# A hybrid decoder layer on one core: weights of the first projection summed on chip, norm totals reordered, and ACT's two roundings of a step exchanged

## What is computed

```
h  = rmsnorm(x) * (1 + scale1) + shift1
u, cq, ckv, kr = split(h @ w_in)             # pooling | latents | rotary key
x  = x + gate1 * (concat(pool(u), attention(cq, ckv, kr)) @ w_out)
h2 = rmsnorm(x) * (1 + scale2) + shift2
x  = x + gate2 * (square(relu(h2 @ w_up)) @ w_down)      # width 4096
y  = rmsnorm(x)
```

## Time and profile before

| | us |
|---|---|
| median of 3 runs | 1430.6 (1430.16 to 1432.28) |
| the profiled execution | 1427.27 |
| its span, first to last instruction | 1425.5 |
| mean granted clock of TensorE | 0.965 of full |
| PE busy | 1335.7 (94%) |
| DVE busy | 1020.3 (72%) |
| ACT busy | 676.0 (47%) |
| POOL busy | 428.3 (30%) |

### The profile page before, as it was taken

One profiled execution on the slowest core, in us unless ns is written; L12 is line 12 of the kernel. 1 busy time (PEld: TensorE's weight loads), 2 busy tenths in 40 slices (PEclk: granted clock), 3 DMA queues, 4 the chain that ended last, 5 costly groups with the idle time before them and its releaser, 6 DMA issues. The chain is left out here.

```text
span 1425.5 us, 29271 instructions
## 1 busy us (share of the span) xinstructions
PE 1335.7 (94%) x11700; PEld 1209.0 (85%) x11700; DVE 1020.3 (72%) x1725; ACT 676.0 (47%) x1371; POOL 428.3 (30%) x349
## 2 busy tenths in 40 slices
PE   6999989999989999698889999999999999999987
PEld 4899876666666766598789999999999999999987
DVE  4855766565657764379777797868979698796985
ACT  5421556565512233234556633665346653467344
POOL 0032043222312221444235161432505234163230
PEclk9999999999969999899889999999999999999999
DMA  9712133424666768954037384563647447485204
GB/s 344 275 52 62 78 118 108 135 79 152 195 242 209 252 209 242 259 132 115 17 70 163 102 157 110 117 150 90 148 119 144 123 92 164 98 181 110 40 1 126
DMA packets 95473, 198.88 MB, mean 140 GB/s; under 512 B 14407, under 2 KB 21523, under 8 KB 91107
## 3 DMA queue, kind: packets, MB, share of 16 engines
q0 software_dynamic: 30576, 87.04, 27.3%
q1 hardware_dynamic: 63537, 109.89, 23.5%
q10 hardware_dynamic: 1226, 0.08, 0.1%
HBM read 180.96 MB, written 13.79 MB: 137 GB/s over the span
## 5 line engine op out<-in xcount | busy, mean ns | idle before, releaser
L1321 PE MATMUL psa<-x_hi,w_hi 128*128 128x272 f32 x2016 | 592.9, 294 | 32.9 <-DVE xT L2417 14.1
L1321 PE MATMUL psa<-x_hi,w_lo 128*128 128x272 f32 x2016 | 588.4, 292 | 0.0
L1321 PE MATMUL psa<-x_lo,w_hi 128*128 128x272 f32 x2016 | 587.0, 291 | 0.0
L1321 PEld LDWEIGHTS psa<-x_hi,w_hi 128*128 128x128 f32 x2016 | 387.8, 192 | 37.5 <-issue 27.1
L1321 PEld LDWEIGHTS psa<-x_hi,w_lo 128*128 128x128 f32 x2016 | 387.3, 192 | 0.0
L1321 PEld LDWEIGHTS psa<-x_lo,w_hi 128*128 128x128 f32 x2016 | 386.9, 192 | 0.2
L758 POOL TENSOR_TENSOR w_lo<-quarter,w_hi 128x512 fp32r<-128x512 f32 x168 | 255.4, 1532 | 245.0 <-ACT w_hi L1750 244.7
L1750 ACT ACTIVATE w_hi<-quarter 128x512 fp32r<-128x512 f32 x252 | 156.3, 620 | 0.0
L2417 DVE SCALAR_TENSOR_TENSOR xT<-psa,modT,xT 128x272 f32<-128x272 f32 (+1 forms) x280 | 116.8, 470 | 0.0
L1773 ACT ACTIVATE x_hi<-t_sum 128x544 fp32r<-128x544 f32 x72 | 47.6, 661 | 120.1 <-PE psa L1321 92.3
L1773 ACT ACTIVATE x_hi<-t_tmp 128x544 fp32r<-128x544 f32 x71 | 47.0, 662 | 88.6 <-PE psa L1321 73.9
(11 more groups left out here) (326 smaller groups left out, 2354.6 us busy)
## 6 DMA issues: line engine op xcount, KB each, us to landing
quarter<-in_w_down POOLq DMA_DIRECT2D x21, 1024.0 KB, 10.2
quarter<-in_w_up SPq DMA_DIRECT2D x20, 1024.0 KB, 5.4
quarter<-in_w_down SPq DMA_DIRECT2D x20, 1024.0 KB, 5.6
quarter<-in_w_up POOLq DMA_DIRECT2D x20, 1024.0 KB, 10.4
wmod<-in_w_mod SPq DMA_DIRECT2D x8, 2048.0 KB, 8.2
wm<-in_w_mod SPq DMA_DIRECT2D x4, 2048.0 KB, 20.5
quarter<-in_w_out POOLq DMA_DIRECT2D x6, 1024.0 KB, 10.0
quarter<-in_w_out SPq DMA_DIRECT2D x5, 1024.0 KB, 9.1
```

Source lines behind the costliest of these rows:

```text
L1321: mm = pe.matmul(tail_bank(p, i)[:, 0:HB], a[:, i * P:i * P + P], x[:, HB * p:HB * p + HB], start=(m in OPENS and k == 0 and q == 0), stop ...
```

## The change

It does these things.

1. M3's weights in stage 0: buffer 5 gets A12+A11 alone (one accumulating load in place of three), and POOL adds buffer 0 (A21+A22) to it in four pieces, `w_sum`, behind w_lo of steps 3, 4 and 5; ACT's w_high of M3 waits for them. A11 is added to buffer 0, for M6, behind the last of them.
2. SP's order of loads: buffers 1 and 3 come later, behind x_back, and buffer 5 ahead of buffer 2.
3. The totals: PE sums into banks 0 and 1, which needs two banks empty in place of eight, and makes the step's other units before the two that take those banks. In the last phase the first step comes ahead of the totals, and the turning of tiles moves back by one.
4. DVE: t_begun for stage 0 too; add_squares(2) at step 31 in place of 28.
5. ACT: `high(j)` calls w_high(j) first and x_high(j) second.

```diff
+PARTS[0][5] = ('A12', 'A11')
...
-    def wait_weights(eng, w, m):
+    def wait_weights(eng, w, m, k):
...
-        if len(ADDED[m]) == 1:
+        if w == 0 and m == 'M3':
+            eng.wait_ge(sem("w_sum"), BEFORE["w_sum"] + k + 1)
+        elif len(ADDED[m]) == 1:
...
         sp.wait_ge(sem("pv5"), 20)
         load_weights(0, 0)
-        sp.wait_ge(sem("pv5"), 24)
-        load_weights(0, 1)
         sp.wait_ge(sem("s5_mm"), HALVES - 2)
         sp.dma_start(wuv_all[:, :, :], w_uv.rearrange("(k p) n -> p k n", p=P)).then_inc(sem("wuv_in"), 16)
-        sp.wait_ge(sem("pv5"), 25)
-        load_weights(0, 2)
         sp.wait_ge(sem("pv5"), 26)
         load_weights(0, 5)
-        sp.wait_ge(sem("pv5"), NPAIR * NB)
-        load_weights(0, 3)
+        load_weights(0, 2)
         sp.wait_ge(sem("oT_mm"), NB)
         x_back(0, 1, 0)
         x_back(1, 0, 0)
         sp.wait_ge(sem("at_mm"), 1)
+        load_weights(0, 1)
         x_back(2, 0, 1)
         x_back(3, 1, 1)
+        sp.wait_ge(sem("pv5"), NPAIR * NB)
+        load_weights(0, 3)
...
+        def w_sum(k):
+
+            g.wait_ge(sem("added_in0"), BEFORE["added_in0"] + 16)
+            g.wait_ge(sem("added_in5"), BEFORE["added_in5"] + 16)
+            g.tensor_tensor(quarters[5][:, k, :], quarters[5][:, k, :], quarters[0][:, k, :], ALU.add).then_inc(sem("w_sum"), 1)
...
         add_weights(0, 0, 1)
         add_weights(0, 5, 1)
-        add_weights(0, 5, 2)
         for j in range(STAGES * STEPS):
             w, pos, k, m = place(j)
             if not LOW_ON_DVE[j]:
                 w_low(j)
-            if j == 1:
-                add_weights(0, 5, 3)
+            if j == 3:
+                w_sum(0)
+                w_sum(1)
+            if j == 4:
+                w_sum(2)
+            if j == 5:
+                w_sum(3)
+                wait_low(g, 3)
+                g.wait_ge(sem("w_sum"), BEFORE["w_sum"] + 4)
+                add_weights(0, 0, 2)
...
-            if ORDERS[w] is LATE and m == 'M5':
+            if w and ORDERS[w] is LATE and m == 'M5':
...
-                if k == 0 and p == 0 and i >= 2 and phase in (6, 8):
-                    pe.wait_ge(sem("n_root"), phase // 2 - 2)
...
-        def total(n):
+        def step_with_total(j, n):
 
+            phase = j // 4
             pe.wait_ge(sem("n_sum"), n + 1)
-            pe.wait_ge(sem("unit_kept"), 8 * (6 + 2 * n))
+            pe.wait_ge(sem("unit_kept"), 8 * (phase - 1) + 2)
             for e in range(2):
                 c0 = HT * n + HB * e
-                mm = pe.matmul(bank(6 + e)[:, 0:HB], ones[:, :], h_all[:, 0, c0:c0 + HB], start=True, stop=True)
+                mm = pe.matmul(bank(e)[:, 0:HB], ones[:, :], h_all[:, 0, c0:c0 + HB], start=True, stop=True)
             mm.then_inc(sem("n_total"), 1)
+            wait_low(pe, j)
+            pe.wait_ge(sem("x_low"), j + 1)
+            for i in (2, 3):
+                pe.wait_ge(sem("unit_kept"), 8 * (phase - 1) + i + 1)
+                unit_part(j, 1, i)
+            for i in range(4):
+                pe.wait_ge(sem("unit_kept"), 8 * (phase - 1) + 4 + i + 1)
+                unit_part(j, 0, i)
+            pe.wait_ge(sem("n_root"), n + 1)
+            unit_part(j, 1, 0)
+            return unit_part(j, 1, 1)
...
         last = STAGES * STEPS - 4
+        step(last, 1)
         pe.wait_ge(sem("unit_kept"), 8 * (last // 4))
         tile_totals(0)
-        for k in range(4):
-            step(last + k, 1)
-            if k == 1:
+        for k in range(1, 6):
+            if k < 4:
+                step(last + k, 1)
+            if k == 2:
                 pe.wait_ge(sem("n_root"), 3)
...
         def high(j):
+            w_high(j)
             x_high(j)
-            w_high(j)
...
-                if w < 2:
+                if w == 1:
                     chain(tt(t2, b12, b22, ALU.subtract))
...
-            if w < 2 or m != 'M1':
+            if w == 1 or m != 'M1':
                 return
-            if w % 2 == 0:
+            if w == 0:
+                v.wait_ge(sem("at_mm"), 1)
+            elif w % 2 == 0:
...
-            if j in (20, 24, 28, 32, 244, 248):
-                add_squares((20, 24, 28, 32, 244, 248).index(j))
+            if j in (20, 24, 31, 32, 244, 248):
+                add_squares((20, 24, 31, 32, 244, 248).index(j))
```

More of the change, by code:

```diff
@@ L114 @@
           "g_row_in": "consts", "y_left": "left", "y_right": "right", "h_scaled": "n_t", "h_done": "h_ready",
-          "t_begun": "n_hi", "samples_kept": "tok_root", "g_done": "turned_hi", "left_mm": "turned", "right_mm": "turned_lo"}
+          "t_begun": "n_hi", "w_sum": "split", "samples_kept": "tok_root", "g_done": "turned_hi", "left_mm": "turned", "right_mm": "turned_lo"}
 BEFORE = {name: 16 for name in SHARED}
 BEFORE.update({"added_in0": 0, "added_in5": 0})
-BEFORE.update({"quarter_in5": 128, "added_in2": 64, "added_in3": 64, "added_in4": 48, "x_back0": 64, "x_back1": 64, "y_left": 9, "y_right": 9, "h_scaled": 25, "h_done": 25, "t_begun": 25, "samples_kept": 9, "g_done": 9, "left_mm": 9, "right_mm": 9})
+BEFORE.update({"quarter_in5": 128, "added_in2": 64, "added_in3": 64, "added_in4": 48, "x_back0": 64, "x_back1": 64, "y_left": 9, "y_right": 9, "h_scaled": 25, "h_done": 25, "t_begun": 25, "w_sum": 10, "samples_kept": 9, "g_done": 9, "left_mm": 9, "right_mm": 9})
 def place(j):
@@ L1378, in _ @@
         for j in range(4, 4 * (7 * STAGES - 1)):
[L1379 to L1384, removed]
+            if j in (24, 32):
+                mm = step_with_total(j, j // 8 - 3)
+            else:
+                step(j, 1)
+                mm = step(j, 0)
             if j % 4 < 3:
@@ L1410, in _ @@
         last = STAGES * STEPS - 4
+        step(last, 1)
         pe.wait_ge(sem("unit_kept"), 8 * (last // 4))
         tile_totals(0)
-        for k in range(4):
-            step(last + k, 1)
-            if k == 1:
+        for k in range(1, 6):
+            if k < 4:
+                step(last + k, 1)
+            if k == 2:
                 pe.wait_ge(sem("n_root"), 3)
[L1417 to L1426, removed]
+            if k > 2:
+                pe.wait_ge(sem("y_right"), BEFORE["y_right"] + k - 2)
+            turn_right(k - 1, *FINAL[0][k - 1])
+            if k > 2:
+                pe.wait_ge(sem("y_left"), BEFORE["y_left"] + k - 2)
+            turn_left(k - 1, *FINAL[0][k - 1])
         pe.wait_ge(sem("y_right"), BEFORE["y_right"] + 5)
@@ L1748, in w_high @@
                 act.wait_ge(sem("pv5"), RING_PAIRS[0][j])
-            wait_weights(act, w, m)
+            wait_weights(act, w, m, k)
             act.activation(w_hi[j % 4][:, :], w_piece(j), ACT.Copy).then_inc(sem("w_high"), 1)
@@ L1813, in root @@
                 act.wait_ge(sem("h_scaled"), BEFORE["h_scaled"] + 8)
-            act.activation(rr[:, 0:HB], bank(6)[:, 0:HB], ACT.Sqrt, bias=eps[:, :], scale=1.0 / D)
-            act.activation(rr[:, HB:HT], bank(7)[:, 0:HB], ACT.Sqrt, bias=eps[:, :], scale=1.0 / D).then_inc(sem("n_root"), 1)
+            act.activation(rr[:, 0:HB], bank(0)[:, 0:HB], ACT.Sqrt, bias=eps[:, :], scale=1.0 / D)
+            act.activation(rr[:, HB:HT], bank(1)[:, 0:HB], ACT.Sqrt, bias=eps[:, :], scale=1.0 / D).then_inc(sem("n_root"), 1)
         def shift(half, c):
@@ L2371, in x_sum @@
             elif m == 'M6':
-                if w < 2:
+                if w == 1:
                     chain(tt(t2, b12, b22, ALU.subtract))
                 else:
-                    v.wait_ge(sem("t_begun"), BEFORE["t_begun"] + 4 * (w - 2) + k + 1)
+                    v.wait_ge(sem("t_begun"), BEFORE["t_begun"] + 4 * (w - (w > 1)) + k + 1)
                 s = tt(t2, t2, b11, ALU.subtract)
```

## The result

The changed kernel takes 1440.6 us (median of 11 runs beside 11 of the kernel before, 1427.6): ratio 1.0088, 95% interval 1.0066 to 1.0111, or 9 to 16 us slower. Forecast: 1431.5, range 1422 to 1438. The sign of the sum held, but by luck: it was the small difference of two terms of 17 and 18 us, and the 13 us measured are outside the range. One of the 11 runs, of 1836 us with a mean granted clock of 0.65, was in a slow state and is left out of the ratio. The profiled execution took 1443.06 us.

The account below looks back on a forecast made before the run. TensorE, busy 94% of the span, was taken as the bound, losing time only when idle or at the lower clock. Gains of 13.9 and 1.9 against a loss of 16.7 gave +0.9 on 1430.6: 1431.5 us, range 1422 to 1438.

Parts of the forecast that it names:

- the start: Start of the tail: POOL's wait for accumulating loads before w_lo goes, PE's 8.94 us stand with it; gain 11.4 us.
- 1.5 back at the first hand-over: First hand-over between products: DVE begins to empty banks 1.5 us later against PE, losing that much.
- M6: Third product: t_begun moves four subtractions out of DVE's crowded stretch, PE's idle 2.52 us falls to about 0.5; gain 3.1.
- totals: Norm totals: waiting for two banks, not eight, and moving add_squares(2) bring n_root(2) 1.9 us earlier; gain 2.0 us.
- the end: Last phase: step(last,1) fills most of 2.59 us idle while DVE empties banks; gain 1.9 us.
- steady part: Steady tail: weights first on ACT delays x_lo before the emptying of banks; 16.7 us lost, bounds 7.4 to 23.
- weights rounded ahead: Around the norm totals: ACT has rounded weights before it must wait for x_sum; gain 0.5 us.
- the two cases of the steady part: Third-step hand-overs: w_lo on DVE, 17 of them, 6.3 us; w_lo on POOL, which blocks x_lo, 19, 10.4 us.
- Rival 1: Steady part: POOL is not first, no collision, cost 7.4 us; net -8.4, 1422 us; chance 0.14.
- 2 (the ring absorbs it): Steady part: steps are rounded three ahead, so no delay reaches PE; net -15.8, 1415 us; chance 0.08.
- Rival 4: Start: another wait replaces the 8.9 us, PE stands as now; about +10, 1441 us; chance 0.08.
- Rival 3: Hand-overs into M6 and M7 of even stages: DVE becomes the bound, +6.4, 1438 us; chance 0.18.

Follow-up runs that it names:

- e1: Changed kernel with ACT's two roundings back in the old order (activations, then weights): 1405.2 us, ratio 0.9837; run again 1408.9 us.
- e6: Changed kernel with ACT's old order and the old totals (banks 6 and 7, eight banks waited for, add_squares(2) at step 28): 1412.5 us, ratio 0.9892.
- e4: Changed kernel, weights first kept, but in each product's third step POOL makes w_lo only after DVE's x_lo: 1416.6 us, ratio 0.9917.
- e11: Changed kernel with ACT's old order, third-step w_lo all on POOL, and M1's third-step t_begun behind the emptying from stage 2 on: 1399.8 us, ratio 0.9816.
- e9: Changed kernel with ACT's old order and, in each product's third step, all w_lo on POOL: 1403.9 us, ratio 0.9845.
- e7: Changed kernel with ACT's old order and the old end (totals ahead of step(last,1)): 1408.4 us, ratio 0.9865.

## Why the prediction was wrong

The forecast set two large terms against each other. The gain was nearly right and the loss far too small: forecast +0.9, measured +13.6 by the tail.

- **The parts other than the order.** By my steps 9.9 at the start (11.4 less 1.5 back at the first hand-over), 3.1 (M6), 2.0 (totals) and 2.4 at the end (1.9, and the 0.5 that I gave to the later x_lo): 17.4 us. e1 shows 18.4. One by one: start 9.3, M6 3.1, totals 3.9, end 2.5. The start has a wait of 1.56 for x_lo(2) where I had gaps under 1 us. The 1.5 back came out right by luck: I had it as DVE late at the first hand-over, but PE's idle there is 2.64 us in e1 as before, and what comes back is the stretch at the lower clock in M3 behind it. The totals were undersized: I took them as a root 1.9 us earlier, but around them PE waits 12.9 us in e1 (1.90, 2.73, 2.35, 2.70, 3.19) and 15.9 in e6 (4.47, 5.60, 3.86, 2.01).
- **The order.** By my steps 16.7 in the steady part, 1.2 before it (0.55, 0.55, 0.35 and 0.25, less 0.5 for weights rounded ahead) and 0.5 at the end: 18.4. e1 against the changed kernel shows 32.0. The failed step is this one, the order's cost, and in it most of all the 1.2 us ahead of stage 2; the 13.6 missed here, less the 1.0 of the parts, is the miss of 12.6 to 12.7.
  - *Steady part, 20.9 in place of 16.7.* The mechanism held to the letter: POOL first, x_lo at 1.30, end 0.58 behind POOL's, all hand-overs that DVE empties without slack, those that ACT empties untouched. e4 splits it into 12.7 of hold-up (forecast 10.4 less 1.1, so 9.3) and 8.3 of lateness (forecast 7.4). The slack was read a little too large: a pair of stages costs 5.73 us and not 4.75. M6 of stage 2 costs 0.92 (I had 0.56), M3 of an odd stage and the M2 behind it 0.3 each (I had 0.17), M6 of odd stages 0.35 (0.2); M7 and M4 cost 0.86 (0.8), M5 0.59 (0.56).
  - *Before stage 2, 8.8 in place of 1.2.* I priced only hand-overs, by the two cases of the steady part, and even credited 0.5 for weights rounded ahead. But weights rounded ahead let POOL start in the middle of DVE's chains, and the rows at 714.71 and 720.88 show two such hold-ups ahead of the 5.08 us gap, where the order costs 1.9. In the whole stretch 17 us of DVE's time have moved into x_lo. PE's idle time carries 4.5 of the 8.8 us, and its busy time, with about 10 us more at the lower clock, the rest. I had no term for either. That hold-ups cause all of the 8.8 us is not shown; e4, which takes them out of the third steps, gives 4.7 to 6.2 of it back.
  - *The end, 2.2 in place of 0.5*: no row was read for it, and its cause stays open. e4, with weights first, has 49.9 us there, so holding POOL back in the third steps is enough to win it back.
- **Rivals.** Rival 1 (POOL not first) and 2 (the ring absorbs it) are refuted by the x_lo row at 844.35 and the steady stretch. Rival 4 (the start fails) is refuted: 10.6 us are there at the end of step(3,1), which ends 15.7 us after attention and 26.25 before. That its number, 1441, is what was measured is chance. Rival 3 named the right engine, with +6.4, but its place (the hand-overs into M6 and M7 of even stages) is not where the loss is (entering M6 and M7 costs 0.92 and 0.86, and not 0.8 more than forecast); over half of what I missed lies ahead of stage 2.
- **The rule weighed.** The Trainium skill (SBUF — State Buffer, section "SBUF: two separate sides") says that whichever of a GpSimd operation and a DVE operation with two SBUF inputs starts first blocks the other for the whole instruction. The runs agree, with one measured detail: the DVE operation ended 0.58 us behind POOL's end whether it had started 0.1 us after POOL (788.65 and 788.73) or 0.57 after (843.78 and 844.35). By that rule it was open to me to ask it of every DVE operation with two SBUF inputs, and I asked it of the x_lo of 19 hand-overs.

## What to carry to other kernels

Where two engines hold each other up, the order in which a third releases them can decide who pays, here 32 us of 1440: release first the one whose work is on the path, or give the other an explicit wait. Such a cost is to be looked for at every operation of the held-up engine from which the bound engine is fed, and first of all in chains without slack (a norm, a start), not only in the steady pattern where it is easiest to read. A "ready sooner" for the engine off the path is no gain by itself: it may be what puts it ahead.

## What the runs showed that I had not expected

- The hold-up depends on the operation. x_lo on two SBUF operands is held up when POOL starts first, but the emptying, one operand in PSUM, keeps 0.43 us where it starts in the midst of POOL's operation (830.30 in the one from 829.92), and POOL's keeps its 1.29. So POOL's work can be put there for nothing; e4 and e11 live on it. Two SBUF operands are not the whole condition: the two DVE operations on modT at the start have one operand of 128x36 and took 0.18 us each before, and 1.16 and 1.20 beside w_sum, each ending 0.04 us behind POOL's addition.
- PE's busy time grew by 11.7 us for the same 4874 matmuls at the same clock. When banks come 0.47 us apart (829.83 and 830.30 in e4) and a unit takes 0.37, PE is late at each bank, and the page counts most of that as busy. The count of matmuls per microsecond tells it; the idle time tells less than half.
- The first product behind a stretch of low clock costs 1.5 us more or less for nothing in the code: M7 of stage 1 took 13.6 us from its first matmul to the next product's in e1, at a granted clock of 0.87, and 12.1 in e9 and e7, at 1.00. Terms of that size before stage 2 are not told by one profile.
